# Mixing and hybrid stages run from one hand-written step list per engine, with a second probability buffer

## What is computed

```python
h = h + 0.5 * rms_norm(swiglu(rms_norm(h, g1), ...), g2)      # feed-forward 1
u = rms_norm(h, mix_pre_g)
y_a = short_conv_mixer(...)            # 3 taps
y_b = conformer_conv_mixer(...)        # 31 causal taps, layer norm, silu
y_c = diff_attention_mixer(...)        # 4 heads x 2 maps, alibi bias
y_d = forgetting_attention_mixer(...)  # 8 heads, decay bias
merged = g[0] * y_a + g[1] * y_b + g[2] * y_c + g[3] * y_d
h = h + rms_norm(merged @ w_o, mix_post_g)
h = h + 0.5 * rms_norm(swiglu(rms_norm(h, g3), ...), g4)      # feed-forward 2
```

```python
z = rms_norm_2(x, g_norm) @ w_in       # queries, keys, values, gates of three branches
oa = dense_gqa_blocks(qa, ka, va) * silu(ag)          # 6 heads, axial rope, rms norm of q, k
ob = windowed_sink_gqa(qb, kb, vb, b_sink) * silu(bg) # 6 heads, window 128, a sink
oc = mla_blocks(...) * silu(cg)                       # 4 heads, low-rank q and kv
x = x + concatenate([oa, ob, oc]) @ w_out
```

## Time and profile before

| | |
|---|---|
| median of three runs | 1741.94 us (1741.90, 1741.94, 1747.24) |
| the profiled execution, its own time | 1740.54 us |
| its span | 1738.7 us |
| mean granted TensorE clock | 0.992 |
| instructions | 25127 |
| chain that ended last | PE 75%, DVE 11%, ACT 6%, DVE sequencer 4%, issue 2%, DMA 1% |
| HBM read | 290.2 MB, 168 GB/s over the span |

### The profile page before, as it was taken

One profiled execution on the slowest core, in us unless ns is written; L12 is line 12 of the kernel. 1 busy time (PEld: TensorE's weight loads), 2 busy tenths in 40 slices (PEclk: granted clock), 3 DMA queues, 4 the chain that ended last, 5 costly groups with the idle time before them and its releaser, 6 DMA issues.

```text
span 1738.7 us, 25127 instructions
## 1 busy us (share of the span) xinstructions
PE 1663.3 (96%) x10644; PEld 1492.9 (86%) x10644; DVE 1091.2 (63%) x1269; ACT 806.0 (46%) x1071; POOL 36.0 (2%) x60
## 2 busy tenths in 40 slices
...
GB/s 278 194 176 188 171 219 183 155 145 146 177 186 197 191 185 180 182 211 184 180 172 223 185 159 160 121 169 194 211 192 177 190 152 152 74 90 166 102 74 49
DMA packets 54479, 292.92 MB, mean 168 GB/s; under 512 B 5712, under 2 KB 10208, under 8 KB 27232
## 3 DMA queue, kind: packets, MB, share of 16 engines
...
...
HBM read 290.23 MB, written 1.06 MB: 168 GB/s over the span
## 4 chain that ended last, share of the span: by engine, by line
PE 75%; DVE 11%; ACT 6%; DVEq 4%; issue 2%; DMA 1%; POOL 0%; ACTq 0%; SPq 0%; POOLq 0%
PE ps L1539 22%; PE ps L1541 22%; PE ps L1540 22%; DVE wlo L1013 4%; ACT whi L647 3%; DVEq L1300 2%; PE ps L2002 1%; DVEq L1214 1%; DVE mix L1209 1%; PE ps L2028 1%; ACT prob L856 1%; PE ps L1637 1%; DVE small L1301 1%; PE ps L1682 1%; ACT tmp L650 1%
## 5 line engine op out<-in xcount | busy, mean ns | idle before, releaser
L1013 DVE TENSOR_TENSOR wlo<-raw,whi 128x2048 fp32r<-128x2048 f32 (+2 forms) x270 | 603.6, 2243 | 400.4 <-ACT whi L647 393.3
L1539 PE MATMUL ps<-xhi,whi 128*128 128x256 f32 (+1 forms) x2000 | 570.1, 285 | 0.0
L1540 PE MATMUL ps<-xlo,whi 128*128 128x256 f32 (+1 forms) x2000 | 565.8, 283 | 0.0
L1541 PE MATMUL ps<-xhi,wlo 128*128 128x256 f32 (+1 forms) x2000 | 565.8, 283 | 0.0
L647 ACT ACTIVATE whi<-raw 128x2048 fp32r<-128x2048 f32 (+2 forms) x270 | 498.6, 1868 | 12.4 <-DMA raw<-stream 11.0
L1539 PEld LDWEIGHTS ps<-xhi,whi 128*128 128x128 f32 (+1 forms) x2000 | 381.9, 191 | 4.5 <-issue 0.9
L1540 PEld LDWEIGHTS ps<-xlo,whi 128*128 128x128 f32 (+1 forms) x2000 | 382.0, 191 | 3.1
L1541 PEld LDWEIGHTS ps<-xhi,wlo 128*128 128x128 f32 (+1 forms) x2000 | 381.9, 191 | 0.5
L1539 PE MATMUL ps<-whi,yar 128*128 128x512 f32 x620 | 246.8, 398 | 2.4 <-DVE yar L1525 1.6
L1540 PE MATMUL ps<-wlo,yar 128*128 128x512 f32 x620 | 241.9, 390 | 0.0
L1541 PE MATMUL ps<-whi,yar 128*128 128x512 f32 x620 | 241.5, 390 | 0.0
...
## 6 DMA issues: line engine op xcount, KB each, us to landing
raw<-stream SPq DMA_DIRECT2D x210, 1024.0 KB, 4.8
...
mix<-cum ACTq DMA_DIRECT2D x2, 1024.0 KB, 4.6
...
```

The source lines that it names most:

```text
L1013: TT(wlo[:, s, 0:w], raw[:, s, 0:w], whi[:, s, 0:w].bitcast(F32), ALU.subtract).then_inc(lo_v, 1)
L1539: pe.matmul(dst, lh, rh, start=first, stop=False)
L1540: pe.matmul(dst, lh, rl, start=False, stop=False)
L1541: return pe.matmul(dst, ll, rh, start=False, stop=last)
```

## The change

The lists become three for each stage, one per engine: `MIX_PE`, `MIX_ACT`, `MIX_DVE` and `HYB_PE`, `HYB_ACT`, `HYB_DVE`. A step has a position (a number), and each engine's list is sorted by it. Splits are steps of their own, and steps in which engines did different things get a name for each: in the hybrid layer `max`, `exp`, `copy`, `o_copy`, `flip_copy`; `a_norm` becomes `a_square` (ACT), `a_mean` and `a_rotate` (DVE, a step for each half of the tokens), `b_rotate` has a step for each half, `o_gate` becomes `o_gate`, `o_high`, `o_low`. POOL's part is written out without a list, in the same order. Every list has the same steps as before; what differs is their order.

The moves:

- PE, mixing: none. PE, hybrid: `scores 3` before `turn 2`, and `values 2` behind the half chunk (9, 1) instead of before it.
- ACT, mixing: splits 14, 15, 16, 17 each before the take of chunk 14, 15, 16, 17 instead of behind it, split 18 before the take of chunk 18, split 19 and split 20 before the takes of 19 and 20; `f_load` and split 23 before the exponentials of group 3; split 25 before the tanh of gate 0 and before `turn 3`; split 26 before `o_norm`.
- ACT, hybrid: split 12 before `exp 2` (before: behind the takes of chunk 9); `o_high 0` before `o_copy 5`.
- DVE, mixing: split 6 before three `conv`; `scores 0` before split 16, `scores 1` before split 18, `values 1` before split 21 and `weigh 2`; `conv (9, 1)`, `(11, 1)`, `(13, 1)` a little later, `(23, 1)` and `(24, 1)` each one split earlier.
- DVE, hybrid: `weigh 0` before split 8; split 9 behind `a_rotate`; split 10 behind `max 2`; `max 4` between the two `b_rotate`; `max 9` before `gate 3`.

The same source in pieces (new names, buffers, waits, ACT's loop):

```diff
-    at(15, "a_split")
-    at(35, "ln_stats")
...
+    at(act, (0.55, 1.55, 2.55, 3.55, 4.55, 5.55, 6.55, 7.55, 8.55, 9.55, 10.55, 11.65, 12.65, 13.55, 14.3494, 14.55,
+             15.55, 16.55, 17.55, 19.232, 19.55, 21.55, 22.55, 23.35, 24.35, 24.4185, 25.35, 27.55, 28.55, 29.55, 30.55,
...
+    return [[x[1:] for x in sorted(e, key=lambda x: x[0])] for e in (pe, act, dve)]
+
+MIX_PE, MIX_ACT, MIX_DVE = mix_steps()
...
         mix = sb("mix", [P, 11456])
+        at = nc.sbuf_base
         yar = sb("yar", [P, 6, KH * T], F32R)
+        probT_b = nc.alloc_sbuf_tensor_at("probT_b", [P, 8, P], F32, offset=at)
...
         def prob2(g):
 
-            return prob
+            return (prob, gpost[:, :].rearrange("p (e k) -> p e k", e=4))[g % 2]
+
+        def probT2(g):
+
+            return (probT, probT_b)[g % 2]
...
-                for step in MIX:
-                    kind = step[0]
-                    if kind == "cols":
-                        i = step[1]
+                for kind, n in MIX_ACT:
+                    if kind == "split":
+                        split(ch + AT_COLS + n + AHEAD)
+                    elif kind == "take":
+                        i = n
...
-                        split(c + AHEAD)
...
-                    elif kind == "values":
-                        g = step[1]
+                    elif kind == "o_copy":
+                        g = n
...
                     elif kind == "exp":
-                        g = step[1]
+                        g = n
                         br, t, kv, ne = group(g)
+                        if g > 1:
+                            act.wait_ge(pt_done, l * GROUPS2 + (8 * DEPTH + g - 1))
...
-                    elif kind == "turn":
-                        g = step[1]
+                    elif kind == "copy":
+                        g = n
                         ne = group(g)[3]
                         act.wait_ge(pt_done, l * GROUPS2 + (8 * DEPTH + g + 1))
-                        if g:
-                            act.wait_ge(o_done, l * GROUPS2 + (8 * DEPTH + g))
-                        A(probT[:, 0:2 * ne, :].rearrange("p a q -> p (a q)"), banks(6, 2)[:, 0:2 * ne * P],
+                        if g > 1:
+                            act.wait_ge(o_done, l * GROUPS2 + (8 * DEPTH + g - 1))
+                        A(probT2(g)[:, 0:2 * ne, :].rearrange("p a q -> p (a q)"), banks(6, 2)[:, 0:2 * ne * P],
                           ACT.Copy).then_inc(pt_ready, 1)
```

More of the change, by code:

```diff
@@ L164, with at @@
 GROUPS1 = 8
+COLS_V = (2, 3, 6, 7)
+COLS_TAKEN = tuple(i for i in COLS if i not in COLS_V and i != 20)
 def mix_steps():
[L168 to L177, removed]
-    at(15, "a_split")
-    at(35, "ln_stats")
[L180 to L202, removed]
+    pe, act, dve = [], [], []
+    def at(engine, slots, kind, numbers=None):
+        for n, slot in zip(numbers or range(len(slots)), slots):
+            engine.append((slot, kind, n))
     chunks = [("cols", i) for i in COLS]
@@ L205, in mix_steps @@
         for half in range(2):
[L206 to L221, removed]
+            chunks += [("gate", (b, half, 0)), ("gate", (b, half, 1)), ("out", (b, half))]
+    for slot, (kind, n) in enumerate(chunks):
+        pe.append((slot + 0.5, kind, n))
+    at(pe, (9.02,), "f_turn")
+    at(pe, (12.02,), "f_sum")
+    at(pe, (35.02,), "ln_stats")
+    at(pe, (37.02,), "ln_back")
+    at(pe, (17.02, 19.04, 21.04, 23.04, 25.06, 27.04, 29.04, 31.04), "scores")
+    at(pe, (19.02, 21.02, 23.02, 25.04, 27.02, 29.02, 31.02, 33.02), "turn")
@@ L239 @@
 GROUPS2 = 10
-SLOTS2 = ((6.5, 7.5), (7.5, 8.5), (9, 9.5), (9.5, 10), (10, 10.5), (10.5, 11), (11, 12), (12, 12.5), (12.5, 14), (14, 14.5))
+TAKES = tuple((p, t) for p, (name, i) in enumerate(HCOLS) for t in range(NT) if name in ("uq", "ukv") or name in Z_PAIRS and i)
 def hybrid_steps():
[L244 to L279, removed]
-            steps.append(("chunk", half // 2, *HCOLS[half // 2], half % 2))
-        else:
-            steps.append(("out", half - 2 * AT_WOUT))
-    assert not before, before
-    return steps
@@ L287, with at @@
-HYB = hybrid_steps()
+    pe, act, dve = [], [], []
+    def at(engine, slots, kind, numbers=None):
+        for n, slot in zip(numbers or range(len(slots)), slots):
+            engine.append((slot, kind, n))
+    for p in range(AT_WOUT):
+        for half in range(2):
+            pe.append((p + half / 2 + 0.4, "chunk", p, half))
+    for n in range(4):
+        pe.append((AT_WOUT + n / 2 + 0.4, "out", n))
+    at(pe, (3.52,), "l_turn")
+    at(pe, (6.02, 6.52, 6.54, 6.56, 9.02, 9.04, 10.52, 10.54), "flip")
```

326 lines of the change are left out of this document (187 added, 139 removed).

## The result

Four runs of the changed kernel gave a median of 1721.15 us (1720.54 to 1722.26), four of the kernel before 1743.81 (1741.9 to 1747.24): a ratio of 0.9882, 95% interval 0.9867 to 0.9897. The profiled execution took 1720.55 us with a span of 1718.8, 19.9 less than before. The forecast was 1722.0. The interval lies clear of 1; the gain is between 1.0 and 1.3%.

The account below looks back on a forecast made before the run. PE was taken as the bound, busy 1663 of 1738.7 us. Mixing 16.2 and hybrid 3.7 made 19.9 off the profiled 1740.5, so 1720.6, and with 1.4 for the median 1722.0; range 1716 to 1731.

Parts of the forecast that it names:

- ACT in the mixing stage: Mixing stages: earlier splits on ACT shorten PE's waits for DVE, winning 5.8 us in stage 0 and 7.4 in stage 1.
- What stays: Each mixing stage: PE waits expected to remain, 1.0 us at turn 2, 1.8 at turn 4, 0.6 at turns 6 and 7.
- split 21 would stay: Mixing stages: DVE's wait at split 21 remains, since scores 2 still stands before that split on ACT.
- fill part of the idle time: Mixing stages, DVE: L1331, moved up, fills part of DVE's idle time; no size of its own.
- The clock: Both mixing stages: the 3.4 us at half clock in each goes, 1.5 us won each, 3.0 together.
- That rival (0.16): Mixing stages: remaining waits at turns 2 and 4 still bring half clock once per stage, 3.0 us more, 1725.0; chance 0.16.
- Hybrid, 2.4 + 2.8: Hybrid stages: PE's waits for weigh and b_rotate shrink, winning 2.4 us in layer 0 and 2.8 in layer 1.
- The second flip's wait: Hybrid stages: the second flip no longer waits, as b_rotate 0 is done a max earlier; 0.8 and 1.1 us before.
- The new wait, 0.75 a layer: Hybrid layers: with max 9 before gate 3, PE's out 0 waits for the gate, 0.75 us lost in each layer.
- The buffers, nothing: Hybrid layers: the second buffers win nothing, since ACT's own list already keeps each exp behind the copy before.
- Edits at nothing: POOL's written-out list, the f_load DMA, DVE's split 6 and ACT's o_high 0: each taken to change nothing.
- the 1 us in hand: Mixing stages, ACT: chunks land 4.8 us after issue, early splits stand 5.7 behind, leaving about 1 us before ACT waits.

Follow-up runs that it names:

- e4: The changed kernel with DVE's mixing list in the old order; ACT's new mixing list and the hybrid part stay: 1719.81 us, ratio 0.9883.
- e7: e4 with split 21 put ahead of the exponentials of group 2 on ACT: 1719.09 us, ratio 0.9886.
- e5: The changed kernel with ACT's mixing list in the old order; DVE's mixing moves and the hybrid part stay: 1730.99 us, ratio 0.9952.
- e3: The changed kernel with the second probability buffers taken away in the hybrid layers, all lists as changed: 1721.0 us, ratio 0.9888.
- e6: The changed kernel with gate 3 before max 9 again in DVE's hybrid list: 1721.71 us, one time.
- e2: The changed kernel with ACT's and DVE's mixing lists in the old order, so the hybrid lists alone: 1734.59 us, ratio 0.9967.
- e10: e7 with three conv taps fewer ahead of values 3 in DVE's mixing list, put in later: 1713.03 us, ratio 0.9842.
- e9: The changed kernel with copies 5, 6 and 8 ahead of splits 13, 14 and 16 in ACT's hybrid list: 1718.54 us, ratio 0.9873.

## Why the prediction was right, point by point

The total was right to 0.9 us, and in part by luck. In the profiles the mixing stages gave 15.1 us for 16.2, the hybrid stage 6.0 for 3.7, and stretches that the change doesn't touch gave back 1.1 for nothing: errors of about 2.3 us up and 2.2 down offset each other. The base moved too: the kernel before ran at 1743.81 us in the same round, not 1741.94, so by the medians the gain is 22.7 us for the 19.9 of the forecast.

1. *ACT in the mixing stage, 5.8 and 7.4.* The mechanism is shown by e4: ACT's moves alone give the shorter stages. What stays was under-sized: forecast 1.0 at turn 2, 1.8 at turn 4 and 0.6 behind, 3.4; measured 1.6, 2.2 and 0.6 in stage 0 (4.4) and 1.3, 2.6 and 0.6 in stage 1 (4.5). So the waits win 4.8 and 6.3. At turn 2 PE was free at 345.8 for the 346.2 of the forecast, and DVE ready at 347.46 for 347.2; at turn 4 PE was free at 374.7 for 374.6, and DVE ready at 376.95 for 376.4. The term that was mis-sized is the residual, a difference of two forecasts of which each was off by 0.1 to 0.6 us. That split 21 would stay was right; e7 shows with DVE's old list that turn 2 waited for it.
2. *DVE's moves* had no term of their own; the text let them "fill part of the idle time". e4 and e5 show that they are worth 3.9 us without ACT's moves and nothing beside them.
3. *The clock, 3.0.* The mixing stages won 15.1 us, the waits 11.1 of it. The two falls that the profile before had, and the one after has not, are worth up to 1.7 each: 3.4, so 0.6 has no name. The size was about right, but the reason was not. "With 1.8 us of wait left, or none, I expect the fall to go" holds for this one profile; in e3 and e6 the same wait of 2.2 or 2.6 brought the fall. That rival (0.16) was no separate case but a thing that happens in some executions of the same mixing lists, for 1.0 to 1.1 us. The four executions of the changed kernel, too, had mean granted clocks of 0.993 to 0.995 and spans of 1718.7 to 1720.4 us. And a fall need not cost anything. These are windows of e4, behind turn 2 in stage 0 and in stage 1:

```profile
347.70:351.10 3.40, 3.40 (x13) 2.32 (x12) 3.25 (x4) 1.41 (x2) 0.00 (x0) 0.50 0.76 248
1045.00:1048.40 3.40, 2.31 (x15) 1.71 (x16) 3.07 (x8) 2.59 (x4) 0.00 (x0) 1.00 0.80 267
```

The first has the half clock, the second has not. In stage 1 turn 4 then waits 1.6 us for DVE, in stage 0 it doesn't wait at all, and both stages stand to the changed kernel's as 225.0 to 225.2 and 226.0 to 226.2. The slow PE used up a wait that it would have had. The same holds of the kernel before: stage 0, with the fall ahead of the flip, took 232.0 us, as e2's with two falls ahead of waits (231.9). The windows of those two, behind turn 2 and at turn 4:

```profile
349.70:353.10 3.40, 3.40 (x14) 2.18 (x12) 3.25 (x5) 0.60 (x1) 0.00 (x0) 0.51 0.48 193
380.40:383.80 3.40, 3.15 (x14) 2.68 (x16) 1.86 (x5) 3.19 (x10) 1.98 (x3) 0.51 0.55 234
```

Taking e2's stages for the old lists, the change gains 6.7 us in each; the 1.7 more in stage 1 were, on this reading, the luck of one execution. The old lists have two such profiles, so this is argued rather than shown.
4. *Hybrid, 2.4 + 2.8.* The second flip's wait went as I said. Those of `weigh` went but for 0.7 in each layer where I had left 0.3: turn 3, which was to start without a wait, still waits 0.4. Layer 0 gained 1.7 net, forecast 1.65. Layer 1 gained 4.3 for 2.05: L2016 went from 2.5 to 0.7, so 1.8 and the 1.1 of the flip, less the gate; the rest is the clock, which I had not counted there. Before, it is at half behind the wait at 1639; first the windows before, then after:

```profile
1639.30:1642.70 3.40, 2.71 (x9) 1.94 (x8) 2.05 (x1) 0.60 (x1) 0.00 (x0) 0.50 0.44 183
1642.70:1646.10 3.40, 3.40 (x10) 2.75 (x10) 1.13 (x2) 1.32 (x6) 0.00 (x0) 0.50 0.00 0
```

```profile
1625.70:1629.10 3.40, 3.40 (x11) 2.74 (x10) 2.25 (x3) 1.81 (x6) 0.00 (x0) 0.50 0.00 0
1629.10:1632.50 3.40, 3.40 (x20) 2.69 (x19) 2.93 (x4) 0.95 (x4) 0.00 (x0) 0.99 0.00 0
```

One stretch of 3.4 us instead of two, worth up to 1.7. The change did nothing to this wait: e2, with the same hybrid lists, has half clock for 6.8 us behind it. PE's idle time alone, from the first exponentials of the stage to the end, fell by 3.8 (32.2 to 28.4), which is the 3.7 of the forecast; the stretch as a whole went from 274.1 us to 267.9. In e4, e7 and e10, which have the new hybrid lists and as much half clock there as the profile before (13.7 us), it takes 268.7 to 268.8.
5. *The new wait, 0.75 a layer.* It is there, ended by L1418, and `out 0` starts 1.89 us behind `values 8` where it started 1.10 behind: 0.79 for the forecast 0.75. But only 0.33 of it is idle time, and taking it away gives 0.3 (e6). The row of PE ahead of those in the earlier trace rows, in the trace before, tells why:

```profile
1555.11 1.56 PE L2028 MATMUL ps<-probT,mix 128*128 128x384 f32 x4 [1.04 <-ACT probT L991]
```

`values 8` ran until 1556.67. The first matmul of `out 0` had started under it at 1556.21 and took 0.69 us, against 0.47 after. I had set the gate's end against that start; against the end of the matmul before, it costs 0.3.
6. *The buffers, nothing.* e3 shows it. The Trainium skill (Perfetto Trace Analysis, Optimization Strategy) reads a repeating gap as possibly too few buffers; here the gaps at L2031 repeat with one buffer and with two, and what ended three of the four was the order on ACT (e9).
7. *Edits at nothing.* Split 24 belongs here: on ACT it has moved from behind the tanh of gate 0 to ahead of it, which the account of the change leaves out; DVE waits for it in neither profile. ACT waited once for a chunk between 309 and 387 us, 1.4 us at 359.78, so the 1 us in hand that I gave the early splits was not enough. It cost nothing: DVE, without a gap from 343.8 to turn 4, came to that split later.
